# Issuing the last 1 MB weight request of a one-core transformer kernel as 16 requests of 8 rows

## The reference

```
N_EXPERTS = 16
EC_CAPACITY = 2
EXPERT_FF = 2 * D_MODEL
...
        x = x + g2 * expert_choice_ffn(h2, router_w[l], expert_w1[l], expert_w3[l], expert_w2[l])
...
    return rmsnorm(x, final_norm_g)
```

## Time and profile before

| | before |
|---|---|
| three runs, median (lowest to highest) | 1363.89 us (1363.01 to 1364.47) |
| profiled execution, its own time | 1364.67 us |
| its span, first to last instruction | 1362.8 us |
| TensorE matmuls, busy | 1050.9 us (77%) |
| VectorE busy | 477.3 us (35%) |
| ScalarE busy | 283.6 us (21%) |
| read from HBM | 484.83 MB, 357 GB/s over the span |
| granted TensorE clock, mean | 0.863 |

### The profile page before, as it was taken

How to read it: one execution, slowest core, us unless ns; L and a number is a source line. 1 busy time by engine, 2 the same in 40 slices (tenths; PEclk the granted TensorE clock), 3 DMA queues, 4 the chain that set the end, 5 groups by cost and what they waited for, 6 DMA issues and landing times.

```text
span 1362.8 us, 16788 instructions
## 1 busy us (share of the span) xinstructions
PE 1050.9 (77%) x7282; PEld 622.6 (46%) x7282; DVE 477.3 (35%) x898; ACT 283.6 (21%) x505; POOL 36.3 (3%) x69
## 2 busy tenths in 40 slices
PE   9999999999999985575675746656585675756677
PEld 8878986799978732132231312313132231313323
DVE  5977777887895311011010111101011010101103
ACT  7547665663264200000000000000000000000002
POOL 0001000000000000000000000000000000000000
PEclk9999999999999998787777878787787777778788
DMA  9755279245437999999999999999999999999995
GB/s 367 302 208 195 75 287 368 96 155 187 185 124 305 409 428 438 433 432 429 435 432 429 435 432 432 430 433 432 433 431 431 432 432 432 431 433 435 429 424 238
DMA packets 23073, 486.96 MB, mean 357 GB/s; under 512 B 2551, under 2 KB 5144, under 8 KB 7000
## 3 DMA queue, kind: packets, MB, share of 16 engines
q1 hardware_dynamic: 22136, 484.31, 84.3%
q10 hardware_dynamic: 864, 1.57, 0.3%
HBM read 484.83 MB, written 1.05 MB: 357 GB/s over the span
## 4 chain that ended last, share of the span: by engine, by line
PE 47%; DMA 44%; DVE 7%; issue 1%; ACT 1%; SPq 0%; DVEq 0%; POOL 0%; ACTq 0%; POOLq 0%
PE ps L282 45%; DMA places<-in_experts 42%; DVE xT L1835 2%; DMA ring<-in_pieces 1%; DVE R L1803 1%; DVE R L1799 1%; DVE ring_r L340 1%; PE ps L1475 0%; PE ps L1847 0%; DVE ring L643 0%; DVE hT_r L560 0%; DVE hT L543 0%; PE ps L1949 0%; PE ps L1120 0%; PE ps L1193 0%
## 5 line engine op out<-in xcount | busy, mean ns | idle before, releaser
L282 PE MATMUL ps<-places,R 128*32 128x512 f32 (+2 forms) x3168 | 454.3, 734 | 271.5 <-DMA places<-in_experts 269.5
L282 PEld LDWEIGHTS ps<-places,R 128*32 128x32 f32 x3168 | 111.2, 133 | 594.5 <-DMA places<-in_experts 309.8
L1796 DVE SCALAR_TENSOR_TENSOR R<-R,ps 128x512 f32<-128x512 f32 x16 | 11.0, 687 | 303.7 <-ACT R L1791 303.7
L282 PE MATMUL ps<-hT_r,ring_r 128*128 128x256 f32 x400 | 113.1, 283 | 0.0
L282 PE MATMUL ps<-U_r,ring_r 128*128 128x256 f32 x480 | 107.7, 284 | 0.4 <-DVE hT_r L560 0.4
L340 DVE TENSOR_TENSOR ring_r<-ring,ring_r 128x2048 fp32r<-128x2048 f32 (+1 forms) x43 | 96.5, 2275 | 21.0 <-ACT ring_r L334 20.9
L1799 DVE SCALAR_TENSOR_TENSOR R<-R,ps 128x512 f32<-128x512 f32 x16 | 11.0, 689 | 225.1 <-PE ps L282 225.1
L282 PE MATMUL ps<-late_r,ring_r 128*128 128x256 f32 x448 | 84.4, 286 | 0.9 <-DVE U_r L572 0.7
L282 PEld LDWEIGHTS ps<-U_r,ring_r 128*128 128x128 f32 x480 | 82.1, 192 | 1.2 <-DVE hT_r L560 1.0
L334 ACT ACTIVATE ring_r<-ring 128x2048 fp32r<-128x2048 f32 (+1 forms) x43 | 79.7, 1896 | 4.1 <-DMA ring<-in_pieces 4.1
L282 PEld LDWEIGHTS ps<-hT_r,ring_r 128*128 128x128 f32 x400 | 76.7, 192 | 0.8 <-issue 0.5
(11 more groups left out here) (367 smaller groups left out, 1086.9 us busy)
## 6 DMA issues: line engine op xcount, KB each, us to landing
places<-in_experts SPq DMA_DIRECT2D x54, 6144.0 KB, 49.6
places<-in_experts SPq DMA_DIRECT2D x29, 2048.0 KB, 18.4
ring<-in_pieces SPq DMA_DIRECT2D x19, 2048.0 KB, 8.6
ring<-in_wmodt SPq DMA_DIRECT2D x8, 2048.0 KB, 8.8
ring<-in_wmodk SPq DMA_DIRECT2D x4, 2048.0 KB, 9.1
ring<-in_pieces SPq DMA_DIRECT2D x4, 1024.0 KB, 9.4
places<-in_experts SPq DMA_DIRECT2D x2, 1024.0 KB, 34.1
ring<-in_pieces SPq DMA_DIRECT2D x1, 1792.0 KB, 12.6
```

Source lines behind the costliest of these rows:

```text
L282: mm = lambda e, o, l, r, st, sp_=True, sk=False: e.matmul(o, l, r, start=st, stop=sp_, skip_group_check=sk)
L1796: e.scalar_tensor_tensor(h, h, 1.0, bank[2 * (ex % 2)][:, :], ALU.add, ALU.mult).then_inc(s["me_h2"], 1)
```

## The change

Request 192, the last, is issued as 16 requests, each for 8 of the 128 partitions (rows p to p + 7, 8 KB each, 64 KB in all), one behind the other on the same queue. They cover the same bytes at the same place. Each adds 16 to the same semaphore, so the count that TensorE waits for rises by 256 where it rose by 16. All other requests keep their form, since for them the loop runs once with all 128 rows.

```
@@ -1719,7 +1719,7 @@
     n = [SLOT_LOADS[i] if i < NSLOT else 0 for i in range(NMOE)]
     for q in range(193):
         if moe_first(q) == q:
-            n[moe_sem(q)] += 16
+            n[moe_sem(q)] += 16 if q < 192 else 256
         MOE_LOADS[q] = n[moe_sem(q)]
 
     def moe_view(q):
@@ -1758,7 +1758,9 @@
             e.wait_ge(s["me_pc"], end_read[q])
         src, at = moe_src(q)
         n = SLOT if q < 191 else SLOT // 2
-        e.dma_start(slots[moe_slot(q)][:, 0:n], src[:, at:at + n]).then_inc(slot_sem[moe_sem(q)], 16)
+        step = 8 if q == 192 else 128
+        for p in range(0, 128, step):
+            e.dma_start(slots[moe_slot(q)][p:p + step, 0:n], src[p:p + step, at:at + n]).then_inc(slot_sem[moe_sem(q)], 16)
```

## The result

The change made the kernel slower: 1368.07 us median of six runs (1367.21 to 1369.83) against 1363.62 us (1363.01 to 1364.47), a ratio of 1.0034 with a 95% interval of 1.0024 to 1.0044. That is outside the range that the prediction gave. The profiled execution took 1369.83 us, with a span of 1367.3 against 1362.8.

A forecast was written before the change was run, and what follows sets the result against it. The weight stream was taken to bound 500 to 1340 us, then TensorE, VectorE and ScalarE in turn. 1364.67 less 0 plus 0 to 0.2 gave 1364.7; with the median 0.8 lower, 1363.9 us, range 1362.4 to 1366.8.

The forecast's parts named there:

- both cases: Request 192's eight engines either finish early, completing it before 1347, or are behind, ending at 1353.0; request 191 stays at 1348.1.
- the second case: Request 192's eight engines are those behind: 4.9 us more after 1348.1, ending at 1353.0, cost 0 to 0.2 us.
- Landing hidden, whichever eight engines take it: Request 192's landing delays TensorE by at most 0 to 0.2 us; time 1363.9 us, chance 0.80.
- slower, by crowding at the destination: Rival: engines writing neighbouring rows into SBUF take multiples of 0.30 us a row; with stuck issue, 1366.7 to 1371.4, chance 0.11.
- late and doubled form: Crowding at SBUF with late engines and doubled row time: request 192 lands at 1357.8, 4.9 us late, time 1368.8.
- the engines are seldom at the same request: Argument against crowding at SBUF: engines of either half run out one by one over 2 us and more.
- I take eight engines: Each 8-row request goes to eight engines, one row each: 16 rows in place of 8, 2.4 us more for them.
- If they are mixed, the latest of the eight decides: If request 192's eight engines are partly early, partly behind, it counts as all behind: cost 0 to 0.2 us.
- the dearest case: Request 192's eight engines are those behind, ending at 1353.0 where TensorE wants it at 1352.95: 0 to 0.2 us.
- The 2.4 us to spare: In the kernel before, request 192 lands at 1350.5 and its matmuls start at 1352.95, so an earlier landing gains 0.
- the 1.5 us named as a sign of being wrong: Stated test: the forecast is wrong if an issue on SP takes over 1.5 us; about 0.43 us each was expected.
- rule that I counted as an estimate: Four neighbouring partitions share one port of about 27 GB/s, so 8 rows reach two ports: 1 MB in 19 us.

The follow-up runs named there:

- e1: Last 1 MB as 8 requests of 16 neighbouring rows in place of the changed kernel's 16 of 8: 1367.18 us, ratio 1.0025 to the kernel before.
- e6: Changed kernel with its 8-neighbouring-row requests all into partitions 0 to 63, rows 0 to 63 read twice, 64 to 127 left out: 1369.38 us, ratio 1.0045.
- e7: Last 1 MB as two requests of 64 rows in place of the changed kernel's 16 of 8: 1367.78 us, ratio 1.0033 to the kernel before.
- e5: Changed kernel with rows 4 partitions apart, all into partitions 0 to 63, rows 0 to 63 read twice, 64 to 127 left out: 1365.46 us, ratio 1.0013.
- e2: Changed kernel with the 8 rows of each of its 16 requests 4 partitions apart: 1367.13 us, ratio 1.0024 to the kernel before.
- e10: The kernel before, unchanged, run once more for a second profile of its tail: 1363.65 us in one run.
- e9: Kernel before with a second 1 MB request of 128 rows ahead of the last one, on its semaphore: 1365.43 us, ratio 1.0013.
- e4: Kernel before with 15 tiny requests of 8 rows of 64 bytes behind the last 128-row request, on its semaphore: 1364.77 us, ratio 1.0008.
- e8: Kernel before with the last 6 MB transfer, requests 183 to 185, issued as three requests of 2 MB: 1363.65 us, ratio 0.9999.
- e3: Changed kernel with the last 1 MB read from a tensor of its own, rows 8 KB apart in place of 48 KB: 1369.17 us, ratio 1.0032.

## Why the prediction was wrong

**The step that failed.** The working holds the landing of request 191 where it was, in both cases: "the others are left with request 191, which lands as now at 1348.1", and "They end request 191 at 1348.1 at the latest". It priced a row of an engine at 0.30 us whatever the others write. Measured, the busy engines moved 16.7 GB/s each in place of 26.6, so a row took about 0.49 us, and request 191 came at 1351.4, 3.4 us later. What the second case adds to it, "16 x 0.30 = 4.9 us more", held: 1351.4 + 4.9 = 1356.3. "Landing hidden, whichever eight engines take it", with its chance of 0.80, fell with the first term.

This is the rival "slower, by crowding at the destination", to which I gave 0.11. Its sign holds. Its late and doubled form, 1368.8, is near the measured 1368.07 by luck: the rows behind request 191 were not doubled, and request 191 itself was late. I had put against it that the engines are seldom at the same request. e1, e6 and e7 show that they crowd all the same, and that engines which are still at earlier requests are slowed as well: request 190 came at 1348.4 in place of 1345.6. I named this for request 191 in half a sentence and gave it no price.

**Who moves the last megabyte.** "I take eight engines" was right: eight completion packets for each request of 8 rows. Of the cases it is the third, "If they are mixed, the latest of the eight decides". In e5 six of the eight are early and two are not, and in the changed kernel the last two rows of counts end at 1354.5 and 1356.3, 5.0 and 4.9 us behind counts for request 191. The sum took the dearest case at 0 to 0.2 us; without crowding e5 measures 1.0013 for it.

e2 and e5 fit best if these eight are the ones that otherwise write partitions 0 to 63. The Trainium skill, "DMA: Bandwidth & Descriptors" (The descriptor swizzle), says this of its engines 0 to 7; the 328 against 176 GB/s of e5 and e2 agree.

**The bottleneck was read rightly, the slack from one execution.** The last landing that held TensorE was that of the last 6 MB transfer, as said. The 2.4 us to spare were those of one execution whose TensorE ran at 1.2 GHz from 1338.4 to 1345.2, and a slow TensorE looks like early transfers. At the full clock it is 0.6 us by e10 and about 0.7 by e9. The granted clock stood in the earlier trace rows, at 0.50, and I passed over it. Alone this would have made the second case, "cost 0 to 0.2 us", about 2 us.

**The issues.** I took 0.43 us each. They cost 0.29 to 1.80 us, which is over the 1.5 us named as a sign of being wrong, and the last went out at 1326.13 in place of 1322.2. That is still 14 us before 1340, so it cost nothing, as predicted. The completion writes, which I put at nothing, come to about 1 us by e4, whose interval runs from -0.1 to 2.2 us.

**What stays open.** The Trainium skill's rule that I counted as an estimate ("SBUF — State Buffer", Door 1: The DMA port swizzle) fits in part. By its figure two engines on one port would move about 13.6 GB/s each, an estimate, and e2 shows 12.8. Its 19 us for 1 MB did not come. Why neighbouring rows slow even the engines that are at other requests is open. The Trainium skill says in "DMA: Bandwidth & Descriptors" (Back-pressure in remote DMA) that a saturated port holds up other engines on the same path. It says so of transfers between cores, and no run here isolates it.

**The sum as it should have been:** request 191 3.4 us later and eight rows more behind it, 2.4 us, give a last landing 5.8 us later. Less 0.6 to 2.4 us of slack this is 3.4 to 5.2 us. Where the clock falls after the wait, as in the profiled execution, 1.1 us come on top, and the range is 3.4 to 6.3 us. The measured median rose by 4.5 us.

## What to carry to other kernels

While other requests are in flight, be wary of cutting a transfer along its partitions. Here requests of 8 or 16 neighbouring rows, and already two requests of 64 rows, cost the running transfers their speed, while the cut of 6 MB into three requests of 128 rows (e8) cost nothing. Count also how many engines a small request goes to: the same eight for all sixteen meant 16 rows for an engine that was behind. Compare GB/s with the DMA share: a share near 1 with half the rate was, here, engines that stood in each other's way. And before calling a wait hidden by two microseconds in a single profile, look at TensorE's granted clock in that stretch, or take a second profile.

## What was not expected of the hardware

- Of 16 DMA engines that were all busy for 840 us, eight finish some 6 us behind the others, in both profiles of the unchanged kernel. The counts in the first trace fall behind on one engine at a time, by 0.6 to 1.6 us, while 16 KB packets of the instruction queue (58 in the run, about 1 us each) are moved. That these hold the eight back was not tried.
- Requests of rows 4 apart ran at 25 to 26 GB/s an engine into partitions 0 to 63 (e5), and at 12.8 into partitions 64 to 127 while the stream was writing there too (e2).
- SP took 0.29 us for a request of 8 rows, but up to 1.80 us in a row of sixteen while the engines had work queued.
- After 1.85 us of waiting TensorE's granted clock went from 1.00 to 0.50 for 3.4 us, which made the stall dearer by 1.1 us. After 1.75 us in e3 it stayed at 1.00.
